# One more buffer for gathered expert rows, and a raw weight ring half as deep, in the first expert stage

## The reference

```
q = (xt @ w_query).reshape(n, PEER_HEADS, 2, PEER_DKEY // 2)
s = einsum('nhmd,mkd->nhmk', q, sub_keys)          # top-16 of each half, then top-16 of 16 x 16 sums
eidx, gate = ...                                   # 128 experts a token, and their softmax weights
act = gelu(einsum('nd,nhkd->nhk', x_blk, expert_u[i_blk]))
out = einsum('nhk,nhkd->nd', g_blk * act, expert_v[i_blk])
```

## Time and profile before

| what | us |
|---|---|
| median of three runs | 4477.61 (4474.81 to 4485.69) |
| the profiled execution, its time | 4473.86 |
| its span | 4472.1 |
| PE busy over the span | 4227.6 (95%) |
| POOL busy over the span | 2620.1 (59%) |
| DVE busy over the span | 2681.6 (60%) |
| ACT busy over the span | 1514.5 (34%) |

### The profile page before, as it was taken

How to read it: one execution, slowest core, us unless ns; L and a number is a source line. 1 busy time by engine, 2 the same in 40 slices (tenths; PEclk the granted TensorE clock), 3 DMA queues, 4 the chain that set the end, 5 groups by cost and what they waited for, 6 DMA issues and landing times. The chain is left out here.

```text
span 4472.1 us, 78888 instructions
## 1 busy us (share of the span) xinstructions
PE 4227.6 (95%) x29672; PEld 4044.1 (90%) x29672; DVE 2681.6 (60%) x4354; ACT 1514.5 (34%) x2455; POOL 2620.1 (59%) x2018
## 2 busy tenths in 40 slices
PE   6899997998998998999899999999799999999999
PEld 5799987887887997999899999999799999999899
DVE  4377765664334313779476667654488888777721
ACT  3122223444443323223233334333333333333332
POOL 5588862222222443446566676667689888777543
PEclk9899998999998999999999999999899999999999
DMA  4333332335974432324589999979899999998532
GB/s 116 90 99 100 100 102 86 107 109 185 375 278 145 123 108 87 98 91 135 183 314 344 326 342 334 335 274 325 319 385 394 395 391 397 350 386 346 227 103 94
DMA packets 363491, 1016.94 MB, mean 227 GB/s; under 512 B 45410, under 2 KB 118882, under 8 KB 300418
## 3 DMA queue, kind: packets, MB, share of 16 engines
q1 hardware_dynamic: 262130, 547.92, 36.4%
q0 software_dynamic: 52192, 370.71, 21.6%
q10 hardware_dynamic: 48944, 95.31, 5.7%
HBM read 931.95 MB, written 79.17 MB: 226 GB/s over the span
## 5 line engine op out<-in xcount | busy, mean ns | idle before, releaser
L252 PE MATMUL rt_acc<-xn_act,rt_w_hi 128*128 128x384 f32 x4096 | 1056.4, 339 | 36.3 <-POOL rt_w_rest L242 35.9
L2795 PE MATMUL val_y_ps<-val_wt,val_v 128*128 128x352 f32 x6144 | 997.0, 323 | 36.5 <-DVE val_wt L2870 28.3
L2795 PEld LDWEIGHTS val_y_ps<-val_wt,val_v 128*128 128x128 f32 x6144 | 986.0, 189 | 46.8 <-issue 44.8
L242 POOL TENSOR_TENSOR rt_w_rest<-rt_w_raw,rt_w_hi 128x512 fp32r<-128x512 f32 x576 | 738.4, 1307 | 492.7 <-ACT rt_w_hi L237 490.4
L252 PEld LDWEIGHTS rt_acc<-xn_act,rt_w_hi 128*128 128x128 f32 x4096 | 742.3, 189 | 51.4 <-POOL rt_w_rest L242 47.8
L2738 POOL TENSOR_TENSOR val_v<-val_v_raw,val_v 128x1024 fp32r<-128x1024 f32 x256 | 613.9, 2410 | 148.9 <-ACT val_v L2826 146.7
L252 PE MATMUL rt_acc<-xn_act,rt_w_rest 128*128 128x384 f32 x2048 | 695.4, 340 | 0.0
L2639 DVE CUSTOM_DVE_ANT_0 rt_space<-rt_space,rt_mid 128x2048 f32<-128x2048 f32 x160 | 361.2, 2282 | 240.1 <-DMA rt_space<-in_peer_u,out_row_id 234.0
L2882 DVE SCALAR_TENSOR_TENSOR val_row_ps<-val_rows,val_row_w,val_row_ps 128x2048 f32<-128x2048 f32 x189 | 444.2, 2350 | 0.0
L237 ACT ACTIVATE rt_w_hi<-rt_w_raw 128x512 fp32r<-128x512 f32 x576 | 334.9, 627 | 289.5 <-PE rt_acc L252 184.6
L2905 DVE TENSOR_TENSOR all_xT<-all_xT,val_y_ps 128x352 f32<-128x352 f32 x512 | 265.2, 518 | 225.2 <-PE val_y_ps L2795 222.2
(11 more groups left out here) (447 smaller groups left out, 7381.5 us busy)
## 6 DMA issues: line engine op xcount, KB each, us to landing
rt_w_raw<-in_peer_uT SPq DMA_DIRECT2D x512, 256.0 KB
val_v_raw<-in_peer_vp SPq DMA_DIRECT2D x128, 1024.0 KB
scan_w_raw<-in_w_in SPq DMA_DIRECT2D x128, 256.0 KB
att_w_raw<-in_w_in SPq DMA_DIRECT2D x96, 256.0 KB
hid_scratch<-rt_hid ACTq DMA_DIRECT2D x128, 192.0 KB
val_hid<-hid_scratch SPq DMA_DIRECT2D x32, 768.0 KB
gate_scratch<-rt_space ACTq DMA_DIRECT2D x11, 2048.0 KB
val_gate<-gate_scratch SPq DMA_DIRECT2D x32, 704.0 KB
```

Source lines behind the costliest of these rows:

```text
L242: e.tensor_tensor(self.rest[:, s, 0:nk, :], self.raw[:, r, 0:nk, :], self.hi[:, s, 0:nk, :].bitcast(F32), ALU.subtract).then_inc(self.rest ...
L252: mm = e.matmul(acc[:, h, 0:width], w[:, s, k, :], act[:, kt0 + k, a, col + h * width:col + (h + 1) * width], start=first and k == 0 and w ...
L2795: mm = e.matmul(y_ps[:, t % 2, 0:VTOK], v[:, c % 2, a, j, t * P:(t + 1) * P], wt[:, g % 2, j, b, :], start=j == 0 and a == 0 and b == 0, s ...
```

## The change

The gathered rows of `peer_u` get four buffers instead of three. The ring of raw weight units in this stage goes from eight slots to four. The scratch area `space`, which holds the row buffers, grows by 2048 floats a partition (8 KB), and the raw ring shrinks by four slots of 2 KB a partition (8 KB), so the stage's memory stays the same size. `VROWS`, the number of row buffers of the second expert stage, stays.

```
-ROWS, VROWS = 3, 5
+ROWS, VROWS = 4, 5
...
     with Space(nc, "rt") as s:
-        w = Stream(s, 2 * RING)
+        w = Stream(s, RING)
...
-        space = s.sb("space", [P, 14336])
+        space = s.sb("space", [P, 16384])
```

## The result

The changed kernel takes 4515.66 us (median of 4 runs, 4507.50 to 4519.93) against 4477.91 us (4 runs). The ratio is 1.0081, with a 95% interval of 1.0069 to 1.0093: 37.8 us slower. The forecast was 4517 us. The sum came out closer than its two terms, and the loss lies in other places than the working had it, as the experiments show. The profiled execution is the shortest of the four, 4507.50 us.

A forecast was written before the change was run, and what follows sets the result against it. The prediction took PE to bound the gathering stage. It added +50 us for the ring and −10 us for the fourth buffer to the profiled 4473.86 us, 4514, plus 3.7 us to the median: 4517 us, range 4472 to 4585.

The forecast's parts named there:

- The view of what bounds the kernel: Gathering stretch: PE bounds it, a faster gather can give back at most 38 us, and SP's ring is always full.
- The ring's term, +50 us: Raw weight loads while rows are gathered: four slots make the round trip 0.5 us too long, 103 times, +50 us.
- the sum of the average round trip: One slot from remainder to next remainder: issue, landing, rounding, remainder and extras make 10.1 us against 9.74 for four units.
- The issue and the landing in it: Raw weight load in the round trip: 0.50 us from remainder to issue's end, then about 6.0 us to land.
- The copy of the product: ACT, once a tile of four units, before the rounding: 0.49 us and 0.7 us behind it, in the round trip.
- the third rival: ACT's queue writes make loads land later than 6.0 us: 7.0 us with one in every trip, +143, 4620 us; chance 0.18.
- The clock: PE's granted clock: if PE's pauses bring it down, as with 0.93 in the first window, the cost grows; no size given.
- The fourth buffer, −10 us: Gathered rows: a fourth buffer takes nearly all of POOL's 43.2 us of dot-product waits away, worth −10 us on PE.
- I take half: PE's 19.9 us of waits for POOL: half was taken as the fourth buffer's gain, −10 us, between 0 and 19.9.
- The rule on turns between queues: DMA engines alternate queues by packet, so a load waits behind at most one gather packet and the fourth buffer doesn't lengthen landing.
- the shallow ring covers all: Rival at the same loads: landings under 5.6 us make the ring cost 0, the buffer wins, 4464 us; chance 0.08.
- the two cancel: Rival at the same loads: landings of 5.7 us or so cost +10 against −10, 4478 us; chance 0.12.

The follow-up runs named there:

- thin gathers: Gathers bring 256 of 2048 floats a row: kernel before (ring eight, three buffers) 4473.7 us; changed kernel (ring four, four buffers) 4448.5 us.
- the half remainder: Changed kernel with POOL computing the remainder for only two of a unit's four blocks in the gathering stretch: 4506.9 us, ratio 1.0060.

## Why the prediction was right, and where it was not

**The view of what bounds the kernel** held. PE bounds the stage, the ring is always full, and DVE's 133.5 us of waits for rows cost nothing: with thin gathers and the old buffers they fell to 42.9 us, and the time did not move.

**The ring's term, +50 us,** measured +52.7 us with three buffers and 59 us with four. The size was right and the working was not, so this was luck. The step that failed is the sum of the average round trip, 10.1 against 9.74 us, times 103 trips. It said that the loss is spread evenly and that each microsecond of the trip is worth 103 us. The issue and the landing in it, 0.33 + 6.0 us, were near: 6.6 us away from the stores. What stood around them was too much, 3.8 us where the trace has 2.7. The copy of the product, 1.2 us, comes once in four units and was charged to every trip. So the trip fits away from the stores, at 9.4 us. Behind them it does not, with landings of 10.0 us and a trip of 12.4: in the changed kernel PE is idle 41.0 us in the 18 us behind the ten stores, where the kernel before has 6.4, and 1.9 us in the rest, where that kernel has 16.2. The loss is where a store of 2 MB and the gathers meet the loads. That mechanism stood in the prediction as the third rival, the writes of ACT's queue. There it was priced as if a write fell into every trip, and with its small writes counted like the large one. It happens once in 32 units.

**The clock** stood in the text as a danger of that rival, without a number. It is some 10 of the 37 us, and with the store in two halves nearly all of it is gone.

**The fourth buffer, −10 us,** gave 14 us with the shallow ring and 19 us with the deep one. The step that failed is "I take half": of PE's 19.9 us of waits for POOL all but 3.9 us stood behind waits for dot products, so nearly the whole upper bound is the answer with the deep ring. The mechanism was right, and POOL's wait fell from 43.2 us to none. That the term was 4 us too small with this ring and the ring's own 3 us too small is why the sum came out so close, which is luck again: +52.7 − 14 = +39 against +50 − 10 = +40.

**The rule on turns between queues** in the Trainium skill, DMA: Bandwidth & Descriptors, section Queues, rings and completion order, fits two measurements and is proven by neither: three or four row buffers leave ACT's waits for landings about the same (237.2 and 242.2 us), and with smaller packets of the store the awaited loads behind it land sooner (8.6 in place of 10.0 us).

**The signs named.** POOL's dot waits under 10 us: they are gone. ACT's waits for landings, 40 to 150 us: 242.2, so this sign missed; most of these waits end before PE needs the unit. PE's wait for POOL near 60 us in the window: 34.8, a miss too. The pace of 2.53 us: 2.52. Nothing before 2180 us and after the stage: 1.8 and 4 us.

**The rivals.** That the shallow ring covers all is true only with thin gathers. That the two cancel is refuted by each edit alone. The late landings came true in part: 10.0 us behind the stores, once in a chunk, and 6.6 us elsewhere. What stays open is the landing of loads for which ACT does not wait, all those of the deep ring among them, which no view gives; and the test of the whole store left out was not made.

## What to carry to other kernels

Size a prefetch ring by the worst stretch in its period and not only by the average round trip: here the average fitted, and the trips failed where a large transfer of another queue met the loads. Look for the biggest store and cut windows behind it, from its first microsecond on. A wait that stands in the queue of an engine in the middle of a stream can reach the bound engine: here 43.2 us of POOL's waits cost 14 to 19 us, and a buffer that removes them is worth memory from elsewhere: here 8 KB from dead columns of another tensor gave 4456.4 us, 21 us under the kernel before. When two edits share one budget, run each alone; this change was a gain of 14 to 19 us and a loss of 53 to 59 us in one.

## What the runs showed of the hardware that I had not expected

Pauses of PE of a few microseconds were followed by stretches at half clock (rows above), worth about 10 us over six stretches, while nearly the same idle time in pauses of at most 2.7 us left one such stretch with the store in two halves. The length of the longest pause does not explain it. With the store in two adjacent transfers pauses of 1.8 to 3.2 us were followed by eight such stretches, and with the half remainder there were ten, seven of them behind pauses of 2.1 to 2.7 us; with 2 KB pieces there were seven. In the changed kernel three pauses of 2.3 to 3.3 us had none behind them. A stretch of the half remainder's kernel, behind a pause of 2.13 us:

```profile
2378.70:2381.90 3.20, 3.20 (x12) 3.01 (x11) 2.00 (x2) 1.26 (x2) 0.79 (x2) 0.50 0.91 361
```

What exactly lets the clock fall was not tested. A 2 MB store delayed awaited 256 KB loads by 0.8 us and cost PE next to nothing when the DMA engines had an eighth of the gathers' bytes to move beside it; with all of them the loads landed 3.4 us later, 10.0 in place of 6.6 us, and PE stood still for up to 4.5 us at once. With half the remainder, where a slot comes free sooner, the awaited landings went from 6.6 to 7.5 us, and the round trip did not change. Cutting the store's packets from 16 KB to 2 KB at the same bytes took PE's idle time from 8 to 18 us behind it from 30.7 to 9.2 us, and that of the first 8 us from 10.3 to 19.4. A second issue of 2 KB pieces on ACT for each chunk cost about 10 us over the stage with the deep ring, some 1 us each.
